# A two-layer diffusion backbone step on one core: layers written out, the close of a layer interleaved with the next projection, and its modulation computed by column strips ahead of time

## The chip, the cores and the metric

The kernel runs on one core of a Trainium2 chip, in float32 throughout but for a few counting matrices. The time is the device time of one launch in microseconds; three runs of the kernel before gave 2504.25, 2508.52 and 2509.11, median 2508.52. Engines: TensorE (PE in the profile) multiplies, VectorE (DVE), ScalarE (ACT) and GpSimd (POOL) work elementwise, SyncE (SP) only issues transfers. ACT and POOL issue transfers too.

## The reference

Two groups of tokens, 512 latent and 128 context, pass through two layers (DEPTH = 2). D_MODEL is 1024. What is computed, in the core of it:

```python
mod = silu(cvec) @ w_mod_l + b_mod_l            # 6 x 1024 values per conditioning vector
sh1, sc1, g1, sh2, sc2, g2 = split(mod, 6)
h = x * (1.0 + sc1) + sh1
qa,ka,va, qb,kb,vb, qc,kc,vc = split(h @ w_in_l)          # 1024 x 3840
oa, ob, oc = diff_attention, neighbourhood_attention, gqa  # latent reads cached context keys too
ga, gb, gc = split(sigmoid(h @ w_gate_l + b_gate_l), 3)
y = (ga * (oa @ w_br[0]) + gb * (ob @ w_br[1]) + gc * (oc @ w_br[2])) @ w_o
x = layernorm(alpha * x + g1 * y)
h2 = x * (1.0 + sc2) + sh2
m = grouped top-2 mixture of 16 experts: sum over chosen e of weight * (silu(h2 @ w1[e]) * (h2 @ w3[e])) @ w2[e]
x = layernorm(alpha * x + g2 * m)
```

Latent tokens are modulated by the vector c, context tokens by c_ctx. Outputs are x of both groups and the context keys and values of both layers.

## The kernel before, in words

The 640 tokens are five tiles of 128 (four latent, the fifth, CTX, context). All weights are cut into pieces of 1 MB (128 x 2048), laid out in DRAM in the order of use, and SyncE streams them into a ring of six slots (`ring`); PE takes each piece in that order and, with some of its matmuls, raises `freed`, which lets SyncE load the piece six places on. The order of work on every engine is that of the code: each engine has its own list, and semaphores (`wait_ge`) tie them.

A first block loads constants and all of x and computes the modulation's first four column groups of 512 (shift and scale of the first sublayer): `open_sp`, `open_pe`, `open_act`, `open_dve`. A group is eight matmuls with the conditioning `cs` as 32 columns of weights, in four column strips of PE's array; the strips hold four *parts of the sum over rows*, so a further matmul with `sel` (L457) adds and turns them into columns. Then a loop over layers (L542) runs one body twice, in blocks with barriers between them:

- `transpose_x` (L756) and `modulate` (L1140) make hT, the modulated transposed input, for all tiles; x is stored to `x_state`, its place is reused, and ACT waits for that store (L1121 is behind it).
- For each of three branches: `project` computes the chunks of the input projection tile by tile (PE line L718 is the shared matmul helper `mm`). Each chunk begins with one more 512-column group of the modulation (`mod_sum`), followed by `mod_rows`, a matmul with `sel` that sums the four strips into two rows, which ACT copies (L1130) and stores to `mrows` in DRAM. Then `attend`, with gate matmuls (`fill`) put between as filler by the table FILL, and `merge`.
- x and the rows come back from DRAM (POOL, L651 to L666) once branch 2's values are mixed. VectorE prepares G1, SH and SC (L1512 to L1519), PE does the output projection by tile, VectorE the residual, statistics and h2 (L1527 to L1537), PE transposes h2 and computes the router.
- Routing on VectorE (L1548 to L1588 up to the choice), rank counting by matmul (L1044), then 17 expert blocks in a pipeline: gather of tokens (POOL), w1, w3, SiLU, w2, store to `y_rows`.
- After a barrier and a possible loop over further blocks, a last block of the layer gathers both outputs of each token (L1794), weighs (L1815), adds (L1827), gates, normalises and, beside it, opens the modulation of `(layer + 1) % DEPTH`. After layer 1 it opens layer 0 again, which nobody reads. x is then stored in one transfer (L1852).

## Time and profile before

| | us |
|---|---|
| median of 3 runs | 2508.52 |
| the profiled execution | 2503.88 |
| its span, first to last instruction | 2502.2 |
| PE busy | 2218.6 (89%) |
| VectorE busy | 882.7 (35%) |
| ScalarE busy | 568.8 (23%) |
| mean granted clock of PE | 0.951 |

PE is the engine that is nearly always busy; an idle microsecond of another engine costs nothing unless PE waits for it. A float32 matmul shows as two instructions in the timelines (x16 for eight matmuls). In a row of a timeline the bracket is the idle time of the engine just before, and what ended it. The granted clock is 1.0 at 2.4 GHz and 0.5 at 1.2 GHz.

### The profile page before, as it was taken

Reading aid. Unit: us, or ns where it says so; the run is one execution under the profiler, and the core shown is the slowest. Engines: PE = TensorE matmul, PEld = TensorE weight load, DVE = VectorE, ACT = ScalarE, POOL = GpSimd, SP = SyncE. Lnnn points to the kernel's source line nnn. Section 1 sums busy time; section 2 is a strip of 40 time slices with the busy share of each in tenths; the row PEclk is TensorE's granted clock in tenths of the full one; section 3 lists DMA queues with packets and bytes.
Section 4 is the critical chain, followed back from the end, with each engine's and each line's share of the span. In section 5 each row is a group of like instructions: output and inputs, shape, how many; then the busy total and the mean of one; then the engine's idle time right before and its main releaser. Section 6 shows DMA issues by size and latency. Waiting matters only on the chain. (4 is left out here: it accounts for less than half of the span.)

```text
span 2502.2 us, 28473 instructions
## 1 busy us (share of the span) xinstructions
PE 2218.6 (89%) x11178; PEld 1408.7 (56%) x11178; DVE 882.7 (35%) x1532; ACT 568.8 (23%) x1040; POOL 242.4 (10%) x245
## 2 busy tenths in 40 slices
PE   3899999999989996999469999999999899969973
PEld 2347754566466643888234576446645665558851
DVE  0115510243543364331532253004435334553216
ACT  2013401142034201122221242113401440112112
POOL 0000010020100000010410001002101000001014
PEclk8999999999999997999679999999999999969985
DMA  8411031211210322799642202211122105059966
GB/s 311 197 78 55 35 105 74 103 47 54 87 68 18 140 105 105 274 364 369 263 186 87 90 34 72 118 72 62 41 88 86 35 18 210 34 192 357 360 267 257
DMA packets 59540, 345.12 MB, mean 138 GB/s; under 512 B 7056, under 2 KB 8208, under 8 KB 28880
## 3 DMA queue, kind: packets, MB, share of 16 engines
q1 hardware_dynamic: 35072, 249.04, 26.3%
q0 software_dynamic: 15744, 63.58, 6.7%
q10 hardware_dynamic: 8592, 30.68, 3.1%
q8 instruction: 91, 1.49, 0.2%
q14 instruction: 41, 0.34, 0.0%
HBM read 309.91 MB, written 37.55 MB: 139 GB/s over the span
## 5 line engine op out<-in xcount | busy, mean ns | idle before, releaser
L718 PE MATMUL ps<-ring,hT 128*128 128x512 f32 (+1 forms) x1280 | 530.1, 568 | 1.1 <-DMA ring<-in_wall 1.0
L718 PE MATMUL ps<-hT,ring 128*128 128x320 f32 x1536 | 464.6, 440 | 0.0
L718 PEld LDWEIGHTS ps<-ring,hT 128*128 128x128 f32 x1280 | 238.2, 190 | 265.9 <-issue 257.2
L718 PEld LDWEIGHTS ps<-hT,ring 128*128 128x128 f32 x1536 | 273.1, 190 | 98.4 <-issue 2.8
L718 PEld LDWEIGHTS ps<-zT,ring 128*128 128x128 f32 x2176 | 255.6, 195 | 18.4 <-issue 15.3
L718 PE MATMUL ps<-zT,ring 128*128 128x128 f32 x2176 | 260.0, 279 | 2.3 <-ACT zT L1283 2.3
L718 PE MATMUL ps<-R,ring 128*128 128x512 f32 (+1 forms) x768 | 211.1, 435 | 4.6 <-DVE zT L1506 3.2
L718 PEld LDWEIGHTS ps<-R,ring 128*128 128x128 f32 x768 | 117.0, 191 | 98.6 <-issue 92.5
L1221 ACT ACTIVATE R<-ps,nmax 128x640 f32<-128x640 f32 x128 | 100.4, 790 | 248.2 <-DVE nmax L1414 248.2
L1414 DVE TENSOR_REDUCE nmax<-ps 128x2 f32<-128x1280 f32 x64 | 95.5, 1491 | 151.4 <-PE ps L842 151.2
L718 PE MATMUL ps<-ring,zT 128*128 128x512 f32 x320 | 139.2, 594 | 3.7 <-DVE zT L1506 3.7
L1394 DVE TENSOR_REDUCE cmax<-ps 128x4 f32<-128x512 f32 x12 | 8.3, 692 | 349.6 <-PE ps L842 349.4
L842 PE MATMUL ps<-R 64*128 64x128 f32 (+3 forms) x992 | 127.5, 383 | 3.1 <-ACT R L1165 1.7
L718 PE MATMUL ps<-ring,R 128*128 128x512 f32 x272 | 122.5, 593 | 3.0 <-issue 3.0
L1237 ACT COPY R<-ps 128x512 f32<-128x512 f32 (+3 forms) x202 | 111.4, 552 | 33.0 <-PE ps L903 26.8
L1678 DVE TENSOR_TENSOR R<-R,ps 128x256 f32<-128x256 f32 x34 | 14.3, 421 | 285.5 <-ACT R L1301 285.5
L842 PEld LDWEIGHTS ps<-R 64*128 64x128 f32 x992 | 92.6, 187 | 37.8 <-issue 14.1
L718 PEld LDWEIGHTS ps<-ring,zT 128*128 128x128 f32 x320 | 60.2, 190 | 76.8 <-issue 72.7
L1183 ACT COPY R<-ps 128x512 f32<-128x512 f32 (+1 forms) x54 | 28.4, 526 | 303.4 <-PE ps L718 303.4
L903 PE MATMUL ps<-ident,R 128*128 128x128 f32 x680 | 91.2, 273 | 6.2 <-DVE R L1435 4.4
L903 PEld LDWEIGHTS ps<-ident,R 128*128 128x128 f32 x680 | 80.2, 141 | 29.2 <-DVE R L1435 6.4
L450 PE MATMUL ps<-ring,cs 128*32 128x512 f32 x192 | 39.1, 939 | 64.0 <-DMA ring<-in_wall 64.0
(195 smaller groups left out, 2012.4 us busy)
## 6 DMA issues: line engine op xcount, KB each, us to landing
ring<-in_wall SPq DMA_DIRECT2D x234, 1024.0 KB, 7.8
y_rows<-R ACTq DMA_DIRECT2D x34, 512.0 KB, 8.7
R<-mrows POOLq DMA_DIRECT2D x16, 512.0 KB, 22.2
R<-in_rows POOLq DMA_DIRECT2D x2, 3072.0 KB, 20.2
x_state<-R POOLq DMA_DIRECT2D x2, 2560.0 KB, 25.1
R<-x_state POOLq DMA_DIRECT2D x2, 2560.0 KB, 12.6
h_rows<-R ACTq DMA_DIRECT2D x10, 512.0 KB, 2.6
R<-in_bias POOLq DMA_DIRECT2D x8, 384.0 KB, 4.2
```

The lines of the kernel that those rows point to most:

```text
L450: last = nc.tensor.matmul(ps[32 * j:32 * j + 32, 6, :], cs[:, 4 * hf + j, :], w[:, j, :], start=hf == 0, stop=hf == 1)
L718: ins = nc.tensor.matmul(out, w, m, start=start, stop=stop, **kw)
L842: return nc.tensor.matmul(out, QT[lo:lo + 64, b, 128 * r:128 * r + 128], KT[lo:lo + 64, key_slot(br, b), k0:k0 + n], start=True, stop=True)
L903: last = nc.tensor.transpose(ps[:, 3 + c + k // 4, 128 * (k % 4):128 * (k % 4) + 128], P[:, i % 2, c, 128 * k:128 * k + 128], ident[:])
L1183: ch.step(nc.scalar.copy(dst, src), a_copy)
L1221: ins = nc.scalar.activation(dst, src, ACT.Exp, bias=nmax[:, n + a:n + a + 1], accum_out=rsum[:, n + a:n + a + 1])
L1237: ch.step(nc.scalar.copy(dst, src), a_pt)
L1394: ch.step(V_.tensor_reduce(m2[:, a, :].unsqueeze(2), s4[:, a], axis=AX.X, op=ALU.max), v_chain)
L1414: ch.step(V_.tensor_reduce(nmax[:, n:n + 2].unsqueeze(2), src, axis=AX.X, op=ALU.max, negate=True), v_max)
L1678: ch.step(V_.tensor_tensor(sig, sig, bank[:, 0], ALU.mult), v_chain)
```

## The change

1. *Layers written out.* `for layer in range(DEPTH)` in Python replaces the loop on the engines; the opening block and the closing block of a layer are gone. What they did stands at the head of the next layer's one big block. The final close is a block of its own, without a modulation.
2. *Modulation by column strips.* A piece of w_mod is now 128 rows by 2048 columns. The four strips of PE's array hold four different groups of 512 *columns*, and eight pieces sum over the rows in place. So no `mod_rows` and no `gsm` copy; ACT stores strips straight to `mrows`. Shift and scale of the first sublayer are one such group of eight pieces, turned into columns by four matmuls (`mod_turn`).
3. *Ahead of time.* Layer 1's first group is computed in layer 0: two pieces before the last transposition of h2, six behind the last router matmul. The first three pieces of layer 1's second group are preloaded.
4. *Close and projection interleaved.* In layer 1, for each tile: gather, weigh, add, normalise, transpose (`transpose_x(t + 1)` inside the matmuls of tile t), modulate, project V (V is now the first chunk of branch 0). The gain and offset of the norm are folded into the modulation columns (`mod_columns`), so x kept in `x_state` is normalised only, and VectorE applies gain and offset when it comes back.
5. *The opening of layer 0* loads x by tile on ACT's queue and modulates hT on VectorE in place.
6. *Other.* x has moved to the space of the gates (its reload waits for the end of `merge(2)`), and the second sublayer's shift and scale are prepared after tile 0's statistics (`second_modulation`). h2 comes by two fused steps without ACT. Sigmoid is replaced by Exp or Tanh. Ranks of routing are accumulated over tiles by matmul. Output x is stored by tile.

The diff, cut to its core:

```diff
-TAIL_FILL = (0, 0, 8)
+TAIL_FILL = (8, 0, 8)
-CHUNKS = {0: (0, 1, 2), 1: (3, 4, 5), 2: (6, 7)}
+CHUNKS = {0: (2, 0, 1), 1: (3, 4, 5), 2: (6, 7)}
+MOD_SPREAD = {0: ((0, 4, 4), (3, 3, 2)), 1: ((3, 3, 2), (3, 3, 2))}
...
+        def mod_strips(k, bank, w, first):
+            for j in range(STRIPS):
+                ins = first if j < STRIPS - 1 else nc.tensor.matmul
+                last = ins(ps[32 * j:32 * j + 32, bank, :], cs[:, k, :], w[:, 512 * j:512 * j + 512], start=k == 0, stop=k == KB - 1)
+            return last
+        def mod_turn(out):
+            for b in range(4):
+                last = nc.tensor.matmul(out[:, 8 * b:8 * b + 8], modraw[:, 128 * b:128 * b + 128], sel[:], start=True, stop=True)
+            return last
...
+        def fetch_and_scale(pool, ch):
+            for t in range(4):
+                fetch_outputs(pool, t)
+            scale_power(pool, ch, 0)
+            fetch_outputs(pool, 4)
+            for t in range(1, NT):
+                scale_power(pool, ch, t)
...
-        with nc.Fori(0, DEPTH) as layer:
+        for layer in range(DEPTH):
...
+                    for i in range(PRELOADED if layer else 0, n_pieces - 3):
+                        if i >= SLOTS:
+                            sp.wait_ge(freed, i - SLOTS + 1)
+                        lay, what = pieces[i]
+                        load(i, lay, WALL.index(what))
...
-                    pool.dma_start(x[:], A["x_state"].rearrange("t p n -> p t n")).then_inc(x_in, 16)
-                    pool.dma_start(rows[:], A["rows"][layer][:, 0:6]).then_inc(rows_in, 16)
+                    pool.dma_start(rows[:], A["rows"][layer]).then_inc(rows_in, 16)
...
+                    spread(G1, 0, g1_in)
+                    pool.wait_ge(v_z, 3 * KB)
+                    pool.dma_start(x[:], (A["x_state"] if layer else A["x"]).rearrange("t p n -> p t n")).then_inc(x_again, 16)
                     spread(SH, 1, g_in)
                     spread(SC, 2, g_in)
...
+                                        if layer:
+                                            pe.wait_ge(a_hT, KB * t + k + 1)
+                                        elif t == 0:
+                                            pe.wait_ge(v_hT, k + 1)
+                                        if layer and k == KB - 3 and t + 1 < NT:
+                                            transpose_x(t + 1, 4)
...
                     router(NT - 2)
+                    if not last_layer:
+                        pe.wait_ge(v_ln, 8)
+                        for k in range(2):
+                            mod_piece(k, 3)
                     transpose_h2(NT - 1)
                     router(NT - 1)
+                    if not last_layer:
+                        for k in range(2, KB):
+                            mod_piece(k, 3)
+                        pe.wait_ge(a_mod, n_mod[0])
+                        mod_turn(ps[:, 4, 384:512]).then_inc(pe_ext, 1)
...
+                    if layer == 0:
+                        act.dma_start(ident[:], A["ident"]).then_inc(ident_in, 16)
+                        for t in range(NT):
+                            act.dma_start(x[:, t, :], A["x"][t]).then_inc(xt_in[t], 16)
+                        act.dma_start(par[:], A["par"][0]).then_inc(par_in, 16)
+                        act.wait_ge(cs_in, 16)
+                        ch.step(nc.scalar.activation(cexp, cs[:], ACT.Exp, scale=-1.0), a_cs)
+                        act.dma_start(zf[:, 0:256 + 2 * NT], A["counting"]).then_inc(count_in, 16)
+                        for n, t in names:
+                            act.dma_start(t[:], A[n]).then_inc(consts_in, 16)
+                        for t in range(NT):
+                            act.wait_ge(pe_xT, 2 * t + 2)
+                            ch.step(nc.scalar.copy(hT[:, :, 128 * t:128 * t + 128], flat(4 * (t % 2), 1024)...), a_raw)
+                        keep_mod(6)
+                    else:
+                        gate_lambda()
+                        weigh(act, ch, 0)
+                        weigh(act, ch, 1)
+                        norm_tile(0)
+                        modulate(0)
...
                     for t in range(NT):
...
                         norm_stats(ch, t)
-                        norm_shift(dve, ch, t, 15)
-                        dve.wait_ge(a_ln, t + 1)
+                        if t == 0:
+                            second_modulation()
...
-                        ch.step(V_.tensor_tensor(h2[:, t % 2, :], x[:, t, :], SC[:, v, :], ALU.mult), v_chain)
-                        ch.step(V_.tensor_tensor(h2[:, t % 2, :], h2[:, t % 2, :], SH[:, v, :], ALU.add), v_h2)
+                        ch.step(V_.scalar_tensor_tensor(h2[:, t % 2, :], x[:, t, :], lnst[:, t, 12:13], SC[:, v, :], ALU.subtract, ALU.mult), v_chain)
+                        dve.wait_ge(g_rs, normed + t + 1)
+                        ch.step(V_.scalar_tensor_tensor(h2[:, t % 2, :], h2[:, t % 2, :], lnst[:, t, 15:16], SH[:, v, :], ALU.mult, ALU.add), v_h2)
```

How the order of instructions moves, at the places that matter. PE at the change of layer, before: what follows the last expert matmul and the skipped loop over further blocks, the opening of the next layer (the rows with `sel` turn a group) and the loop back.

```order
L1783 UNCONDITIONAL_BRANCH
L450 MATMUL ps<-ring,cs 32x512 x8
L457 MATMUL ps<-sel,R 128x2 x4
L450 MATMUL ps<-ring,cs 32x512 x8
L457 MATMUL ps<-sel,R 128x2 x4
L450 MATMUL ps<-ring,cs 32x512 x8
L457 MATMUL ps<-sel,R 128x2 x4
L450 MATMUL ps<-ring,cs 32x512 x8
L457 MATMUL ps<-sel,R 128x2 x4
L1775 UNCONDITIONAL_BRANCH
L542 REGISTER_ALU
L542 COMPARE_AND_BRANCH
```

Now (from the head of layer 1's block; L712 and L451 with `cs` are modulation pieces, L744 transposes x, L712 with `hT` projects V):

```order
L693 UNCONDITIONAL_BRANCH
L712 MATMUL ps<-ring,cs 32x512 x3
L451 MATMUL ps<-ring,cs 32x512
L712 MATMUL ps<-ring,cs 32x512 x3
L451 MATMUL ps<-ring,cs 32x512
L712 MATMUL ps<-ring,cs 32x512 x3
L451 MATMUL ps<-ring,cs 32x512
L744 MATMUL ps<-ident,R 128x128 x8
L712 MATMUL ps<-ring,hT 128x512 x5
L744 MATMUL ps<-ident,R 128x128 x8
L712 MATMUL ps<-ring,hT 128x512 x8
L744 MATMUL ps<-ident,R 128x128 x8
L712 MATMUL ps<-ring,hT 128x512 x8
```

The four modulation groups and the loop's branches are gone from between the layers; three pieces stand first, and each later tile's transposition lies five matmuls into the tile before it.

PE in layer 0 at the end of the output projection, before (L718 with `wr` is the router, L1011 transposes h2, L1044 counts ranks):

```order
L718 MATMUL ps<-ring,zT 128x512 x16
L1011 MATMUL ps<-ident,R 128x128 x8
L718 MATMUL ps<-wr,hT 128x16 x16
L1011 MATMUL ps<-ident,R 128x128 x8
L718 MATMUL ps<-wr,hT 128x16 x8
L1044 MATMUL ps<-selbf,lt 128x80
L1045 MATMUL ps<-selbf,ones 128x80
```

And now: the router of tiles 2 and 3, two modulation pieces, the last h2, its router, then the first of six pieces.

```order
L712 MATMUL ps<-wr,hT 128x16 x16
L712 MATMUL ps<-ring,cs 32x512 x3
L451 MATMUL ps<-ring,cs 32x512
L712 MATMUL ps<-ring,cs 32x512 x3
L451 MATMUL ps<-ring,cs 32x512
L1018 MATMUL ps<-ident,R 128x128 x8
L712 MATMUL ps<-wr,hT 128x16 x8
L712 MATMUL ps<-ring,cs 32x512 x3
L451 MATMUL ps<-ring,cs 32x512
L712 MATMUL ps<-ring,cs 32x512 x3
L451 MATMUL ps<-ring,cs 32x512
```

The pieces stand where PE waited for VectorE before.

VectorE at the start of the output projection, before (the ten 1024-wide rows, then the first of tile 0's residual, L1527 and L1528):

```order
L1514 TENSOR_TENSOR R<-R 128x1024
L1515 SCALAR_TENSOR_TENSOR R<-R 128x1024
L1517 TENSOR_TENSOR R<-R 128x1024
L1518 TENSOR_TENSOR R<-R 128x1024
L1519 TENSOR_TENSOR R<-R 128x1024
L1514 TENSOR_TENSOR R<-R 128x1024
L1515 SCALAR_TENSOR_TENSOR R<-R 128x1024
L1517 TENSOR_TENSOR R<-R 128x1024
L1518 TENSOR_TENSOR R<-R 128x1024
L1519 TENSOR_TENSOR R<-R 128x1024
L1527 SCALAR_TENSOR_TENSOR R<-ps,R 128x512
L1528 SCALAR_TENSOR_TENSOR R<-R 128x512
```

And now:

```order
L1612 TENSOR_TENSOR R<-R 128x1024 x2
L1639 SCALAR_TENSOR_TENSOR R<-ps,R 128x512
L1643 SCALAR_TENSOR_TENSOR R<-R 128x512
L1639 SCALAR_TENSOR_TENSOR R<-ps,R 128x512
L1643 SCALAR_TENSOR_TENSOR R<-R 128x512
L438 BN_STATS R<-R 128x6 x2
L439 BN_AGGR R<-R 128x2
L440 TENSOR_SCALAR small<-R 128x1
L1621 TENSOR_TENSOR R<-R 128x1024
L1622 SCALAR_TENSOR_TENSOR R<-R 128x1024
L1624 TENSOR_TENSOR R<-R 128x1024
L1625 TENSOR_TENSOR R<-R 128x1024
```

The ten rows have moved behind the residual and the statistics of tile 0 (L438 to L440), in front of its h2.

## Rows read from the trace of the kernel before

**Rows 1.** The page, part 1: busy us (share) and instructions of PE.

```profile
PE 2218.6 (89%) x11178; PEld 1408.7 (56%) x11178; DVE 882.7 (35%) x1532; ACT 568.8 (23%) x1040; POOL 242.4 (10%) x245
```

**Rows 2.** Windows view, stretch: length, busy per engine (instructions), PEclk, DMA share, GB/s.

```profile
892.04:1001.41 109.37, 86.26 (x297) 46.76 (x297) 64.71 (x126) 12.78 (x12) 6.30 (x8) 0.87 0.22 80
1001.41:1205.90 204.49, 201.83 (x1430) 168.24 (x1430) 56.49 (x131) 39.93 (x50) 18.54 (x16) 0.98 0.84 317
1205.90:1291.36 85.46, 27.75 (x137) 13.90 (x136) 43.64 (x56) 26.66 (x33) 35.17 (x22) 0.58 0.67 257
2424.46:2502.20 77.74, 20.22 (x97) 8.32 (x96) 42.11 (x50) 15.30 (x15) 34.85 (x21) 0.54 0.64 247
...
10.00:20.00 10.00, 1.93 (x8) 0.20 (x8) 0.45 (x3) 0.00 (x0) 0.00 (x0) 1.00 1.01 419
```

**Rows 3.** PE timeline, opening: start, duration, line, out<-in, count, idle before it.

```profile
65.95 7.54 PE L718 MATMUL ps<-ring,hT 128*128 128x512 f32 x16 [0.98 <-DMA ring<-in_wall]
80.80 1.87 PE L718 MATMUL ps<-R,sel 128*2 128x512 f32 x2 [7.32 <-ACT R L1121]
82.60 8.30 PE L718 MATMUL ps<-ring,hT 128*128 128x512 f32 x16
```

**Rows 4.** ACT timeline, opening (ACTq: its DMA issues).

```profile
14.66 8.80 ACTq L512 DMA_DIRECT2D iota<-in_iota  x1
23.98 0.59 ACT L465 COPY R<-ps 128x512 f32<-128x512 f32 x1 [20.57 <-issue]
```

**Rows 5.** DMA issues of the span: transfer, count, KB each, us to landing.

```profile
R<-mrows POOLq DMA_DIRECT2D x16, 512.0 KB, 22.2
R<-x_state POOLq DMA_DIRECT2D x2, 2560.0 KB, 12.6
h_rows<-R ACTq DMA_DIRECT2D x10, 512.0 KB, 2.6
R<-in_x ACTq DMA_DIRECT2D x1, 2560.0 KB, 23.5
```

**Rows 6.** PE timeline at the layer change.

```profile
1279.51 2.40 PE L756 MATMUL ps<-ident,R 128*128 128x128 f32 x10 [12.11 <-issue]
1291.36 1.92 PE L718 MATMUL ps<-ring,cs 128*32 128x512 f32 x16 [1.83 <-ACT hT L1140]
1300.28 1.02 PE L718 MATMUL ps<-R,sel 128*2 128x512 f32 x2
1301.23 7.13 PE L718 MATMUL ps<-ring,hT 128*128 128x512 f32 x16
```

**Rows 7.** POOL, ACT and DVE timelines at the layer change.

```profile
1212.50 0.98 POOL L1794 DMA_INDIRECT zT<-y_rows,yrow  x1 [41.32 <-issue]
...
1219.55 1.15 ACT L1815 ACTIVATE zT<-zT,R 128x1024 f32<-128x1024 f32 x1 [12.56 <-DMA R<-y_rows,yrow]
...
1223.52 1.28 DVE L1827 SCALAR_TENSOR_TENSOR zT<-R,zT 128x1024 f32<-128x1024 f32 x1 [1.50 <-ACT zT L1815]
1227.36 1.42 DVE L395 BATCH_NORM_STATS2 R<-R 128x6 f32<-128x512 f32 x2
```

**Rows 8.** PE and DVE timelines, start of the output projection of layer 0.

```profile
892.04 27.73 PE L718 MATMUL ps<-ring,zT 128*128 128x512 f32 x64 [1.87 <-DVE zT L1506]
919.61 1.04 PE L1011 MATMUL ps<-ident,R 128*128 128x128 f32 x8
...
897.06 1.23 DVE L1517 TENSOR_TENSOR R<-R 128x1024 f32<-128x1024 f32 x1
915.56 1.23 DVE L1537 TENSOR_TENSOR R<-R 128x1024 f32<-128x1024 f32 x1
```

**Rows 9.** PE timeline, end of the output projection and routing, layer 0.

```profile
975.57 1.97 PE L1011 MATMUL ps<-ident,R 128*128 128x128 f32 x8 [4.04 <-DVE R L1537]
991.57 0.25 PE L1044 MATMUL ps<-selbf,lt 128*128 128x80 bf16 x1 [9.34 <-DVE selbf L1588]
```

**Rows 10.** SyncE timeline, last DMA issue of the span.

```profile
2493.88 0.41 SPq L1852 DMA_DIRECT2D out_y<-R  x1
```

840 lines of the change are left out of this document (426 added, 414 removed).

## The prediction

> **What bounds the kernel now.** I read the page's busy shares first, then cut the span into stages with the windows view, then read each engine's timeline where the cuts show idle time. TensorE (PE) is busy 2218.6 us of 2502.2 [rows 1], so only 283.6 us are to be had unless its work shrinks. In the expert stage it is busy 201.83 of 204.49 us, and the transfers move 317 GB/s there with the engines 84% busy [rows 2]: full, and untouched by the change. The idle time lies in four places: the opening, where the first projection starts at 65.95 us and the second tile only at 82.60 after a 7.32 us wait for ScalarE [rows 3]; the change of layer, 85.46 us with PE busy for 27.75; routing, where PE is busy 86.26 of 109.37 us; and the last 77.74 us, where the 20.22 us of PE work is a modulation for a third layer that is never run [rows 2]. The granted clock is 0.58 and 0.54 in the two gaps against 0.98 in the expert stage [rows 2], that is mostly 1.2 GHz: what PE starts after a gap runs slow at first.
>
> **The opening.** Before, subtracting one steady tile (7.13), one row sum (0.95) and one modulation sum (1.92, durations from [rows 6]) from 82.60 gives 72.6 us as the moment from which the stream would have run without loss. Now: nothing waits for all of x or for a barrier, but 15 transfers are issued on ScalarE's queue before its first copy of x, where there were 12 before its first copy; that copy began at 23.98, after 20.57 us without work, 8.80 of them inside one issue [rows 4]. I put it at 25. Then PE has three tiles to transpose (2.0 each on the slow clock [rows 9]: 6) and seven of the eight modulation pieces left (0.96 each fast, from 1.92 for 16 instructions [rows 6], up to twice that slow; I take 1.2: 8.4), and ScalarE's copy (0.6 [rows 4]), the turn into columns (1.9, priced as the 2-instruction row sum at 1.87 [rows 3]), and small column operations (about 1.7, no row, from six operations at a few tenths): 43.6, say 44. Gain 28.6. Bounds: the data needed is 8.4 MB of modulation, 2.6 MB of x and 1.2 MB of constants, 12.2 MB at 419 GB/s [rows 2] or 29 us, plus start and tail, 37 at best; 52 if ring slots are freed late behind the blocked copies. So 20 to 36.
>
> **Row sums.** Each of eight chunks per layer had a matmul that summed four partial rows; the strips are now whole sums. Start to start it takes 0.95 (1300.28 to 1301.23 [rows 6]), sixteen of them: 15.2, all on PE's path. The modulation sums themselves stay (32 instructions of the same form per 2048 columns) and only change places.
>
> **Second modulation.** This one goes the other way. x now shares its space with the gates, so its reload is issued after the last merge step, with the shift and scale rows queued behind it, and ten 1024-wide VectorE operations on them come after tile 0's statistics. Before they ran at once from 892 on, and h2 of tile 0 was ready at 916.79, 2.8 us before PE wanted it (915.56 + 1.23 against 919.61 [rows 8]). Count from the first output matmul, 892.04: the second half of tile 0 ends at +13.9 (half of 27.73, by two tiles, [rows 8]); add two operations (1.4), statistics (1.9, from 1.42 [rows 7] and two small ones), ten at 1.26 (1.23 and its gap [rows 8]: 12.6), two for h2 (2.6): +32.4. PE wants it at +27.6. It waits 5 us, and restarts on the slow clock (a transposition block is 1.97 after a 4.04 us wait [rows 9] against 1.04 [rows 8]), which I price at 2.5 with the matmuls behind. The reload (12.6 [rows 5]) fits in front of the +13.9; rows from mrows took 22.2 behind 9 MB, now behind 2.6 MB; if they took that again they would land near +24, 7 us late. Per layer 7.5, bounds 0 and 15: cost 15, bounds 0 and 30.
>
> **End of projection and routing.** VectorE now subtracts the mean and scales in two fused steps, so ScalarE's pass over x and its two hops leave the chain of h2 (about 2.1 of the 4.04 us wait [rows 9]); Exp in place of Sigmoid drops a table load, and fewer group operations and rank sums by matmul save some 2.6 more of the 9.34 [rows 9] and what follows. Layer 1 gets this whole, with some slow-clock time back: 8. In layer 0 the eight modulation pieces of layer 1 are put into these waits. Only two are in the ring; six must be loaded once the output weights are freed, and 6.3 MB at 419 GB/s is 15 us, plus about 1.5 of start and finish (h rows: 2.6 us for 0.5 MB [rows 5], which moves in 1.3). They end about 17 us after the loads start, then copy and turn (2.5): just where the rank matmul starts before, 991.57. So layer 0 gains 1. Together 9, bounds 2 and 14.
>
> **The change of layer.** Before, 85.46 us from the last expert matmul to the first modulation sum of layer 1 [rows 2]. Now the gathers start as before (1212.50, +6.6), the first pair is usable at +13.65 (1219.55) [rows 7], but SyncE issues three ring loads at once and three more as PE uses the preloaded pieces. With equal shares the first pair is 2.6 us later and each next one 5 apart; say +17. Scaling 1.15, combine 1.28, two steps of 1.23, statistics 1.9 [rows 7 and 8], the power and the mean (0.8, no row), ScalarE's normalising pass (1.15 like the scaling), half a transposition and one modulate put the first projection matmul near +29 to +31; I take 30. Tile 1 then needs VectorE 6.1 and ScalarE about 5 us per tile against PE's 8.2 (7.13 + 1.04), so the supply keeps up after one wait of some 2.3. Four more transpositions inside the stream cost 4.2; three modulation pieces are done inside the gap, 2.8 saved. 30 + 2.3 + 4.2 - 2.8 = 33.7: gain 51.8, bounds 42 and 58.
> The trace shows that shares need not be equal: x (2.6 MB) took 23.5 us [rows 5] beside ring loads, 112 GB/s of 419. The Trainium skill, DMA: Bandwidth & Descriptors, section Queues, rings and completion order, says that a DMA engine takes turns between queues by whole packets, not by bytes; with 8 KB ring rows against 4 KB gathered rows that gives gathers a third, the trace agrees, and the first rival below is what it would make of this place.
>
> **The end.** Before, 77.74 us after the last expert matmul [rows 2]. Now the dead modulation, its barrier and the 2.5 MB store in one piece (2493.88 to the end, 8.3 [rows 10]) go; per tile VectorE does combine, gate, add, statistics and two fused steps, 1.28 x 3 + 1.23 x 2 + 1.9 + gaps 0.5 = 8.7. First combine at +15.5 (the pair usable at +13.65 as at the layer change, scaling 1.15, and under 1 us for the 1 MB of final rows loaded beside), five tiles 43.5, last store 0.4 + 2.6 [rows 5] + 1: 63. Gain 14.7, bounds 8 and 17.
>
> **Sum.** 28.6 + 15.2 - 15 + 9 + 51.8 + 14.7 = 104.3 from 2502.2: 2397.9 of span. The profiled execution before took 2503.88, 1.7 over its span, and the median of the runs is 4.6 above that (lowest 0.4 above); with half of it, 2401. The rest (Tanh for Sigmoid in the experts, V before Q and K, eight fill matmuls moved to the last K unit, layers written out) I cost at nothing: VectorE is 28% busy under the experts [rows 2], the fills are the same 128 per branch. Were V-first to expose the last K copy, it would be 1 us per layer.
>
> **Rivals.**
> *Starved handover.* While 6.3 MB of ring loads last (some 20 us at 307 GB/s) a pair of gathers, 1 MB, comes every 9.4 us at x's 112 GB/s in place of 5. Two pairs are then late by 4.4 each: the first projection is at +34 and the next tile waits as much again, and the slow clock lasts longer; together 14 more: 2415. For it: the 23.5 us [rows 5]. Against: the ring has only 6 slots, so its lead ends after 6.3 MB. 0.17.
> *Second modulation hidden.* Rows land early and the wait is under 2 us per layer, without slow clock; for it, the 2.8 us of slack before. Against: ten operations in VectorE's line. 2401 - 13 = 2388. 0.15.
> *The opening stays blocked.* ScalarE's queue holds it until x is in (27 us) and the ring, its slots freed late, runs behind: first projection at 55, gain 17.6: 2412. 0.13.
> *The experts turn transfer-bound, slower than before.* Layer 0 enters its experts with the ring behind, and the stage needs 4.2 MB per expert in 11.7 us. The price is 34 periods; the gains of 104 are eaten from 3.1 us per period on, for instance 14.9 us each: 2401 + 110 = 2511. Against: bytes and slots are unchanged and 84% is not full; ring loads run at 2.5 us per MB when not held. 0.02.
> *It does not do what it says*: the projection of layer 1 still waits for the whole close, because the tiles' scaling, normalising and modulation queue on ScalarE in one order. Then the first tile comes after all five, 20 later: 2421. 0.06.
>
> **How the numbers follow.** The forecast, 2401, has 0.47. Ends of all terms together give 2367 and 2450; they will not all fall one way, and 8 in 10 of the cases above lie in 2378 to 2426. What this kernel's measurement can tell from no change is 0.2%, 5 us; every case but the transfer-bound one is far beyond it: faster 0.97, same 0.01, slower 0.02.
>
> **What would show it.** Right: the first ring-by-hT matmul at 40 to 48 us; no matmul of sel by R with 512 columns; one wait of PE of 3 to 8 us for h2 before the first transposition block of each output projection; the first projection of layer 1 28 to 33 us after the last expert matmul of layer 0; an expert stage of 204 to 206 us; an end of 60 to 65 us. Wrong: new waits of PE for the ring in routing or the experts, waits of several us in more than one tile at the layer change, or a granted clock near 0.5 through the first projected chunk, which would cost up to 7 us a tile.

## The result, and the profile after

The changed kernel takes 2436.11 us (median of 4 runs, 2433.51 to 2438.39), the kernel before 2508.82 (2504.25 to 2509.3): a ratio of 0.9714, 95% interval 0.9697 to 0.9731. It is faster by 72.7 us, where the prediction's sum had 104.3. The time lies 35 us above the predicted 2401 and 10 us above the range. The profiled execution has a span of 2435.8 us, PE busy for 89% of it as before, with 38.7 us less work [rows 1]:

```profile
PE 2179.9 (89%) x11018; PEld 1395.5 (57%) x11018; DVE 888.5 (36%) x1519; ACT 530.9 (22%) x1004; POOL 215.4 (9%) x231
```

To see where a forecast of a sum went wrong, both spans are cut at the same events, with the forecast of each stage beside them. The events are the first projection matmul, the first matmul of the output projection, the first expert matmul and the end of the last, per layer; the "before" of the first two lines counts from 72.6 us, as the prediction did, and in layer 1 from the first modulation sum of the first chunk (1291.36), for the same reason. "Forecast" is before with the prediction's terms put in (the sixteen row sums are 7.6 a layer).

| stage, us | before | forecast | measured | missed by |
|---|---|---|---|---|
| opening | 72.6 | 44 | 41.3 | -2.7 |
| layer 0, first to output projection | 819.4 | 811.8 | 830.8 | +19.0 |
| layer 0, output projection and routing | 112.5 | 119.0 | 123.7 | +4.7 |
| layer 0, experts | 201.4 | 201.4 | 200.5 | -0.9 |
| last expert matmul to first projection | 85.5 | 30 | 32.9 | +2.9 |
| layer 1, first to output projection | 819.4 | 815.5 | 825.0 | +9.5 |
| layer 1, output projection and routing | 112.3 | 111.8 | 118.0 | +6.2 |
| layer 1, experts | 201.4 | 201.4 | 201.1 | -0.3 |
| end | 77.7 | 63 | 62.6 | -0.4 |

The new gaps are small, and most are in places where the prediction had seen none. In the windows view (length, busy time per engine, PEclk, DMA share, GB/s) of output projection and routing, the change of layer and the end, which answer to the rows in [rows 2]:

```profile
872.07:981.10 109.03, 98.47 (x353) 49.46 (x354) 56.59 (x90) 5.88 (x7) 11.45 (x11) 0.92 0.39 153
1196.29:1229.14 32.85, 7.03 (x32) 2.59 (x33) 11.39 (x18) 5.26 (x7) 10.74 (x11) 0.62 0.84 333
2373.22:2435.80 62.58, 0.00 (x1) 0.00 (x0) 40.28 (x45) 6.75 (x6) 18.60 (x15) 0.54 0.40 151
```

PE's timeline in the first projection of layer 0 (start, duration, line, out<-in, count, idle before it and its releaser; L774 transposes a Q or K unit):

```profile
38.36 1.06 PE L457 MATMUL ps<-sel,R 128*128 128x8 f32 x8 [0.79 <-ACT R L1151]
41.27 37.47 PE L712 MATMUL ps<-ring,hT 128*128 128x512 f32 x80 [1.85 <-DVE hT L1405]
...
87.27 16.07 PE L712 MATMUL ps<-ring,hT 128*128 128x512 f32 x32 [4.95 <-DMA ring<-in_wall]
...
131.79 8.80 PE L712 MATMUL ps<-ring,hT 128*128 128x512 f32 x16 [2.53 <-DMA ring<-in_wall]
140.43 0.60 PE L774 MATMUL ps<-ident,R 128*128 128x128 f32 x4
140.87 7.03 PE L712 MATMUL ps<-ring,hT 128*128 128x512 f32 x16
```

The stream starts at 41.27, where [rows 3] had 65.95 and 82.60. But it stops twice for weights, 4.95 and 2.53 us. After the second stop eight matmuls (x16) take 8.80 us, after the next unit 7.03. Only what comes right behind the wait is slow.

The same at the change of layer, PE and then ScalarE (ACT L493 weighs a gathered tile, L1178 normalises, L1172 modulates, L1246 copies V):

```profile
1227.38 1.97 PE L744 MATMUL ps<-ident,R 128*128 128x128 f32 x8 [19.52 <-ACT R L1178]
1229.14 5.71 PE L712 MATMUL ps<-ring,hT 128*128 128x512 f32 x10
1236.74 1.07 PE L744 MATMUL ps<-ident,R 128*128 128x128 f32 x8 [1.88 <-issue]
1237.65 7.03 PE L712 MATMUL ps<-ring,hT 128*128 128x512 f32 x16
1246.24 1.07 PE L744 MATMUL ps<-ident,R 128*128 128x128 f32 x8 [1.56 <-issue]
```

```profile
1215.80 1.15 ACT L493 ACTIVATE zT<-zT,R 128x1024 f32<-128x1024 f32 x1 [12.61 <-DMA R<-y_rows,yrow]
1223.20 1.15 ACT L493 ACTIVATE zT<-zT,R 128x1024 f32<-128x1024 f32 x1 [6.24 <-DMA R<-y_rows,yrow]
...
1235.40 1.24 ACT L1178 ACTIVATE R<-R 128x1024 f32<-128x1024 f32 x1 [1.73 <-DVE R L1393]
1237.47 3.90 ACT L1172 ACTIVATE hT<-ps,modcol 128x128 f32<-128x128 f32 x8 [0.83 <-PE ps L744]
1241.40 0.59 ACT L1246 COPY R<-ps 128x512 f32<-128x512 f32 x1
1242.02 1.15 ACT L493 ACTIVATE zT<-zT,R 128x1024 f32<-128x1024 f32 x1
1244.90 1.24 ACT L1178 ACTIVATE R<-R 128x1024 f32<-128x1024 f32 x1 [1.73 <-DVE R L1393]
```

Where [rows 6] had one transposition for all of x at 1279.51 and a projection from 1301.23, tile 0 is projected from 1229.14. ScalarE then needs 9.50 us per tile (1235.40 to 1244.90): 6.88 of work and 2.6 of waiting. PE needs 7.03 + 1.07 less overlap, 7.9, and waits for the difference ahead of three tiles (1.88, 1.56 and 1.56 us; the last one it has in time).

The output projection, VectorE (L1639 and L1643 residual of a half tile, L1621 the first of ten rows of the second modulation, L1654 h2) and PE in layer 0, then PE in layer 1:

```profile
872.05 2.48 DVE L1612 TENSOR_TENSOR R<-R 128x1024 f32<-128x1024 f32 x2
884.80 0.69 DVE L1639 SCALAR_TENSOR_TENSOR R<-ps,R 128x512 f32<-128x512 f32 x1 [10.27 <-DMA R<-in_x]
...
891.21 1.23 DVE L1621 TENSOR_TENSOR R<-R 128x1024 f32<-128x1024 f32 x1
...
905.13 1.28 DVE L1654 SCALAR_TENSOR_TENSOR R<-R 128x1024 f32<-128x1024 f32 x1
```

```profile
906.47 1.97 PE L1018 MATMUL ps<-ident,R 128*128 128x128 f32 x8 [4.97 <-DVE R L1654]
...
2089.71 1.97 PE L1018 MATMUL ps<-ident,R 128*128 128x128 f32 x8 [7.85 <-DVE R L1654]
```

In [rows 8] the ten rows ran from 892 on and h2 was ready in time. Now VectorE stands idle for 10.27 us and does them afterwards.

### The profile page after: what moved, and what is told of

Its sections match the earlier page's. It is cut to its first block and busy times, and to the rows that moved or that the text cites. A ratio compares the mean times of both kernels' runs of the same rounds, so it can differ in the third digit from the quotient of the medians.

```text
span 2435.8 us, 27121 instructions
## 1 busy us (share of the span) xinstructions
PE 2179.9 (89%) x11018; PEld 1395.5 (57%) x11018; DVE 888.5 (36%) x1519; ACT 530.9 (22%) x1004; POOL 215.4 (9%) x231
## 5 line engine op out<-in xcount | busy, mean ns | idle before, releaser
L712 PE MATMUL ps<-ring,hT 128*128 128x512 f32 (+1 forms) x1280 | 536.9, 575 | 13.5 <-DMA ring<-in_wall 7.9
L712 PE MATMUL ps<-hT,ring 128*128 128x320 f32 x1536 | 465.2, 440 | 0.0
L712 PEld LDWEIGHTS ps<-ring,hT 128*128 128x128 f32 x1280 | 241.6, 193 | 274.7 <-issue 258.0
L712 PEld LDWEIGHTS ps<-hT,ring 128*128 128x128 f32 x1536 | 273.3, 190 | 97.8 <-issue 2.5
L712 PEld LDWEIGHTS ps<-zT,ring 128*128 128x128 f32 x2176 | 254.5, 194 | 18.4 <-issue 15.3
L712 PE MATMUL ps<-zT,ring 128*128 128x128 f32 x2176 | 258.9, 279 | 2.3 <-ACT zT L1349 2.3
L712 PE MATMUL ps<-R,ring 128*128 128x512 f32 (+1 forms) x768 | 211.1, 435 | 4.6 <-DVE zT L1606 3.2
L712 PEld LDWEIGHTS ps<-R,ring 128*128 128x128 f32 x768 | 116.9, 191 | 98.6 <-issue 92.5
L712 PE MATMUL ps<-ring,zT 128*128 128x512 f32 x320 | 143.9, 610 | 3.7 <-DVE zT L1606 3.7
L712 PE MATMUL ps<-ring,R 128*128 128x512 f32 x272 | 122.5, 593 | 3.0 <-issue 3.0
L1793 DVE SCALAR_TENSOR_TENSOR R<-R,ps 128x256 f32<-128x256 f32 x34 | 14.3, 421 | 280.3 <-ACT R L1367 280.3
L712 PEld LDWEIGHTS ps<-ring,zT 128*128 128x128 f32 x320 | 62.1, 196 | 79.9 <-issue 75.7
L1246 ACT COPY R<-ps 128x512 f32<-128x512 f32 (+1 forms) x54 | 28.5, 527 | 348.4 <-PE ps L712 348.3
L942 PE MATMUL ps<-R 128*64 128x128 f32 x1088 | 73.5, 279 | 12.9 <-ACT R L1299 12.9
## 6 DMA issues: line engine op xcount, KB each, us to landing
R<-in_x ACTq DMA_DIRECT2D x5, 512.0 KB, 13.5
```

What stands on the lines that cost most here:

```text
L712: ins = nc.tensor.matmul(out, w, m, start=start, stop=stop, **kw)
L942: last = nc.tensor.matmul(ps[64 * a:64 * a + 64, 5, 128 * r:128 * r + 128], V[:, kt, 64 * vh:64 * vh + 64], PT[:, a, 128 * j:128 * j + 128 ...
L1246: ch.step(nc.scalar.copy(dst, src), a_copy)
L1793: ch.step(V_.scalar_tensor_tensor(sig, sig, 1.0, bank[:, 0], ALU.add, ALU.mult), v_chain)
```

## The experiments

Every edit is made on the changed kernel. Ratios are to the kernel before, with 95% interval; the changed kernel itself is at 0.9714 and, run again beside e9 and e10, at 2434.85 us, 0.9709 (0.9694 to 0.9725).

### e1_second: the second modulation into VectorE's idle time

```
                     spread(G1, 0, g1_in)
+                    spread(SH, 1, g_in)
+                    spread(SC, 2, g_in)
                     pool.wait_ge(v_z, 3 * KB)
                     pool.dma_start(x[:], ...).then_inc(x_again, 16)
-                    spread(SH, 1, g_in)
-                    spread(SC, 2, g_in)
...
+                    second_modulation()
                     dve.wait_ge(x_again, 16)
...
-                        if t == 0:
-                            second_modulation()
```

> Edit, alone on the changed kernel: the spreads of the second shift and scale are issued before POOL waits for the last z block, and VectorE does the ten operations of the second modulation before it waits for the x that is loaded again. Theory A (the ten operations sit behind the x load, 12.6 us of VectorE in series with a 10.27 and a 9.05 us idle wait): they move into that idle time, h2 of tile 0 is ready about 10 us sooner in each layer, the PE waits for h2 (4.97 and 7.85 us) and the cold transpositions after them go, about 6 to 9 us per layer; time about 2421, 2417 to 2425. Rival B (what lies between output projection and router is set by VectorE's sum of work or by the x load itself, not by this order): the waits move to later tiles and the time stays within 4 us of 2436. Rival C: the spreads only come so late that VectorE waits for them instead, no gain.

Measured 2418.48 us (5 runs, 2415.05 to 2423.26), 0.9647 (0.963 to 0.9664): 17.6 us less. Theory A. VectorE's timeline shows the ten rows from 874.34 to 886.9, with no wait for x behind them, and PE's transposition of the first h2 no longer waits and takes 1.04 us in place of 1.97:

```profile
885.68 1.22 DVE L1626 TENSOR_TENSOR R<-R 128x1024 f32<-128x1024 f32 x1
886.94 0.69 DVE L1640 SCALAR_TENSOR_TENSOR R<-ps,R 128x512 f32<-128x512 f32 x1
```

```profile
871.84 29.43 PE L712 MATMUL ps<-ring,zT 128*128 128x512 f32 x64 [1.87 <-DVE zT L1606]
901.11 1.04 PE L1018 MATMUL ps<-ident,R 128*128 128x128 f32 x8
```

From output projection to rank matmul the stage falls from 109.0 to 101.7 us in layer 0 and from 107.1 to 96.4 in layer 1. The order of these ten operations had cost 7.3 and 10.7 us.

### e2_late, e3_233, e12_800: where the modulation pieces of layer 0 stand

```
-MOD_SPREAD = {0: ((0, 4, 4), (3, 3, 2)), 1: ...}
+MOD_SPREAD = {0: ((0, 0, 0), (3, 3, 2), (5, 3)), 1: ...}   # e2_late, groups in branches 1 and 2
+MOD_SPREAD = {0: ((2, 3, 3), (3, 3, 2)), 1: ...}           # e3_233
+MOD_SPREAD = {0: ((8, 0, 0), (3, 3, 2)), 1: ...}           # e12_800
```

> Edit, alone: layer 0 takes its two further modulation groups in the projections of branches 1 and 2 (3, 3, 2 and 5, 3 pieces before the chunks) and none in branch 0. Theory A (in the changed kernel the four pieces ahead of the second and third chunk fill the ring beside the two pieces held, so the next chunk's weights land late: waits of 4.95 and 2.53 us and a slow clock after each): both waits and the slow matmuls go, 10 to 13 us less, about 2424 (2421 to 2428). The cost of the modulation matmuls themselves (0.86 us a piece) only moves. Rival B (the projection of branch 0 is slow for want of clock after the opening, whatever the ring does): within 4 us of 2436. Rival C (the five pieces before branch 2's first chunk are loaded late in their turn): a ring wait of 3 to 5 us there, half of the gain lost, about 2430.

Measured 2427.21 us (5 runs), 0.9679 (0.9665 to 0.9693): 8.9 less, theory A's direction and a little short of its 10 to 13, and the pieces' own 6.9 us (8 x 0.86) are still there, in branch 2. No ring wait is left in the first branch's projection. One of 2.29 us stands at the second branch's third chunk, and a ring wait of 3.50 us in the opening, which the changed kernel's trace has at 0.56, put the first projection at 44.6. That start moves by itself: the seven other traces with the changed kernel's opening and projection of the first branch (c_after, e1, e4, e5, e6, e7, e9) have it between 41.96 and 44.44.

> Edit, alone: the modulation pieces in branch 0 of layer 0 stand 2, 3, 3 before the chunks where the changed kernel has 0, 4, 4. Theory A (ring full): the waits inside the projection shrink to under 1 us each, but the first chunk starts 5 to 7 us later, since two pieces load ahead of its weights; net 3 to 6 us less, about 2431. Rival B (the ring is not the cause): 5 us more, 2441, for the later start.

Measured 2424.68 us (5 runs), 0.9684 (0.9666 to 0.9703): 11.4 less, more than theory A gave. The first projection starts 4.3 us later, and first to output projection takes 813.9 us in place of 830.8. Of these 16.9 us, 1.7 are two pieces that stand ahead of it now, and 1.6 lie behind the projection, where the changed kernel's trace has a stretch of slow matmuls behind a wait for ScalarE that most other traces don't have (e8 and e9 do). The remaining 13.5 lie between the first projection matmul and the last but one Q/K transposition (128.4 us against 113.1): 7.0 of ring waits, 3.5 of slow matmuls behind them and 2.9 of slow matmuls in the first chunk. In the eight traces with the changed kernel's order in it this stretch takes 123.5 to 128.4 us, 126.1 in the mean, so against the mean the gain is 11.3. The windows view over the projection of branch 0, the changed kernel first, then two finer cuts of it (PEclk is the third number from the end):

```profile
41.27:78.74 37.47, 37.47 (x84) 16.24 (x88) 5.76 (x16) 5.94 (x12) 0.00 (x0) 0.92 0.26 108
78.74:110.00 31.26, 26.31 (x84) 11.09 (x84) 4.46 (x8) 1.18 (x2) 0.55 (x1) 0.89 0.53 210
110.00:131.79 21.79, 19.26 (x78) 8.32 (x77) 4.47 (x8) 2.96 (x5) 0.00 (x0) 1.00 0.18 67
131.79:152.00 20.21, 20.20 (x49) 9.24 (x50) 4.46 (x8) 1.18 (x2) 0.00 (x0) 0.92 0.57 241
```

```profile
50.00:78.74 28.74, 28.74 (x71) 12.44 (x74) 0.00 (x0) 2.34 (x4) 0.00 (x0) 1.00 0.03 12
110.00:125.69 15.69, 15.69 (x50) 7.43 (x52) 4.47 (x8) 1.55 (x3) 0.00 (x0) 1.00 0.00 0
```

And e3_233:

```profile
45.55:80.20 34.65, 34.65 (x84) 15.24 (x88) 1.87 (x9) 2.55 (x5) 0.00 (x0) 1.00 0.31 129
80.20:110.00 29.80, 29.33 (x92) 12.73 (x86) 6.70 (x12) 1.78 (x3) 0.55 (x1) 1.00 0.47 185
110.00:131.00 21.00, 21.00 (x76) 9.29 (x75) 3.44 (x7) 2.97 (x5) 0.00 (x0) 1.00 0.44 173
```

With two pieces of work just ahead of it the first chunk runs at 2.4 GHz throughout here (1.00), where the changed kernel's first chunk, behind waits of 0.79 and 1.85 us, has 0.92. That this is the pieces' doing is not shown: e8 and e10 have the same two pieces there, and their first chunks took 36.2 and 36.3 us, e3's 34.6, the changed kernel's 37.5. The two finer cuts show the full ring: while PE works through a chunk the transfers stand still (12 and 0 GB/s), and they run at 241 when the weights are needed already. e3's ring waits there are 0.47 us.

> Edit, alone on the changed kernel (undoes 'ahead of time and spread' for layer 0): all eight pieces of the next modulation group stand before the first chunk of layer 0, none between chunks. The pieces land about 2.5 us apart. Theory A (the opening is bound by the ring's loads once ScalarE is free, and ring room is what costs later): the first projection starts 18 to 22 us later, near 61, the waits of 4.95 and 2.53 us and the slow clock inside the projection go (11 us, as e3 and e2 showed); net 6 to 11 us more, 2442 to 2446. Rival B (the loads hide behind the wait for the modulation columns): the first projection starts under 10 us later and the time is below 2435.

Measured 2435.33 us (5 runs), 0.9704 (0.9686 to 0.9721): the same time as the changed kernel, between the two theories. The mechanism is A's, since the first projection starts at 60.39, behind pieces that land one by one:

```profile
47.88 1.08 PE L712 MATMUL ps<-ring,cs 128*32 128x512 f32 x3 [1.42 <-DMA ring<-in_wall]
50.36 1.07 PE L712 MATMUL ps<-ring,cs 128*32 128x512 f32 x3 [0.55 <-DMA ring<-in_wall]
52.84 1.07 PE L712 MATMUL ps<-ring,cs 128*32 128x512 f32 x3 [0.55 <-DMA ring<-in_wall]
...
60.39 50.30 PE L712 MATMUL ps<-ring,hT 128*128 128x512 f32 x112 [0.64 <-DMA ring<-in_wall]
```

The sum in the expectation was wrong. I had left out that the eight pieces' matmuls leave the stream (6.9 us), and priced ring and clock at 11. First to output projection takes 809.4 us, 21.4 less, of which 6.9 are those and 1.6 the slow stretch behind the projection; the 12.9 left are ring waits and slow clock (10.7 against the mean of the eight traces). So all that the changed kernel wins in the opening by putting these pieces off, 19.1 us, it pays back in the projection.

### e4_fill: the gate matmuls ahead of the last K unit

```
-TAIL_FILL = (8, 0, 8)
+TAIL_FILL = (0, 0, 8)
...
-    ((0, 6, 0),) + 6 * ((0, 4, 3),) + 4 * ((0, 4, 2),) + 6 * ((0, 4, 3),) + ((0, 6, 0),),
+    ((4, 6, 0),) + 16 * ((0, 4, 3),) + ((0, 6, 0),),
```

> Edit, alone: the eight gate matmuls that the change put ahead of the last K unit of branch 0 go back to where the kernel before has them (4 ahead of slot 0, and 4 slots with 3 after the transpositions in place of 2). Theory A (those matmuls cover no wait of their size before the attention, and four slots now wait 0.8 us each for want of them): 1 to 3 us less per layer, about 2432 (2429 to 2435). Rival B (they cover the copy and transposition of the last K unit, a wait of 3 to 4 us opens in their place in each layer): 2 to 6 us more, about 2440.

Measured 2430.49 us (5 runs, 2427.23 to 2436.77), 0.9701 (0.9684 to 0.9719): 5.6 less in the medians, but the intervals overlap, so the time alone does not settle it. The traces do: from the last but one Q/K transposition to the first mixing of values it is 16.75 us in place of 19.35, and every trace of a kernel with the eight matmuls ahead has 19.35 or 19.36 there, in both layers. Theory A, with 2.6 us per layer. Eight matmuls (4.47 us together) covered a wait that with the old order is 0.28 us long:

```profile
166.80 0.66 PE L774 MATMUL ps<-ident,R 128*128 128x128 f32 x4 [0.28 <-ACT R L1246]
```

### e5_ring: the ring's loads behind the gathers

```
+                        if layer and i in (3, 5):
+                            sp.wait_ge(yt_in[i - 3], 32)
```

> Edit, alone on the changed kernel: in layer 1 SyncE loads its fourth and fifth ring piece only when the first pair of gathered outputs is in, and the sixth when the third pair is in; in the changed kernel all five loads are issued at the start of the layer, beside the gathers. Theory A (the gathers share the DMA engines with five ring pieces, so pair 0 takes 12.9 us from the start of its gather): pair 0 lands 3 to 6 us sooner and the first projection of layer 1 starts 3 to 6 us sooner (27 to 30 us after the last expert matmul, against 32.85); time 2431 to 2433. Rival B (the gathers are set by POOL's issue of the descriptors, 1.3 us each, or by their own latency): within 1.5 us there and 2 us of 2436 in all. Rival C: the weights come too late in their turn, a ring wait opens ahead of the first projection, 2 to 6 us slower.

Measured 2427.79 us (5 runs), 0.9669 (0.9647 to 0.9691): 8.3 less, more than expected. The last expert matmul ends at 1197.36 here, and the first projection starts at 1222.64, 25.3 us later in place of 32.9. ScalarE's timeline:

```profile
1210.93 1.15 ACT L493 ACTIVATE zT<-zT,R 128x1024 f32<-128x1024 f32 x1 [6.67 <-DMA R<-y_rows,yrow]
1213.94 1.15 ACT L493 ACTIVATE zT<-zT,R 128x1024 f32<-128x1024 f32 x1 [1.86 <-DMA R<-y_rows,yrow]
1219.58 1.24 ACT L1180 ACTIVATE R<-R 128x1024 f32<-128x1024 f32 x1 [4.50 <-DVE R L1395]
```

Pair 0 is usable 13.6 us after the last expert matmul (19.5 in the changed kernel, 13.65 before [rows 7]) and pair 1 3.0 us after it (7.4). No weight is late in the first chunk.

### e6_two, e7_half, e9_nmr: ScalarE's period

> Leaves out: in layer 1 the first modulation takes the gain and offset of column 0 for all 8 column blocks, so that ScalarE does two operations of 128 x 512 in place of eight of 128 x 128 per tile. Theory A (ScalarE's period of 9.49 us per tile sets the first chunk of layer 1, PE needs 7.9): with modulate at about 1.3 us in place of 3.90 the waits of 1.88, 1.56 and 1.56 us ahead of the transpositions go, and the first tile is ready 1 to 2 us sooner; 5 to 7 us less, about 2430. Rival B (the period is set by VectorE's combine chain or by the gathers, ScalarE only has much to do): the tile period stays above 9 us and the time within 2 us of 2436.

```
+                        if layer:
+                            for k in range(2):
...
+                                nc.scalar.activation(hT[:, 4 * k:4 * k + 4, ...], ps[:, 4 + k, :]..., ACT.Identity,
+                                                     scale=modcol[:, KB:KB + 1, v], bias=modcol[:, 0:1, v]).then_inc(a_hT, 4)
```

Measured 2432.36 us (5 runs, 2427.04 to 2434.95), 0.9689 (0.9665 to 0.9713). The medians give 3.7 less, the ratios 6; the interval overlaps the changed kernel's. In the trace modulate takes 1.64 us in place of 3.90 and the tile period falls from 9.50 to 8.57 (1231.64 to 1240.21), the waits from 1.56 to 0.64. They do not go: ScalarE still waits 1.73 us for the mean in every tile, and 1.35 opens before its copy of V. So its work was a part of the period and not the whole: neither theory in full. The time alone cannot tell this run from the changed kernel.

> Edit, alone: in layer 1 VectorE modulates the upper four column blocks of tiles 2, 3 and 4 (four operations of 128 x 128 from PSUM each), ScalarE the rest. Theory A (ScalarE sets the period): the waits ahead of the transpositions of tiles 3 and 4 go and that of tile 2 stays; 2 to 4 us less, about 2433. Rival B (VectorE's own chain of about 7 us per tile then holds the modulation back): the waits turn into waits for VectorE of 2 us or more at tile 2, no gain or up to 3 us more.

```
+SHARED = (2, 3, 4)
...
+                                for u in (SHARED[:-2] if t < NT else SHARED[-2:]):
+                                    dve.wait_ge(pe_xT, 2 * u + 2)
+                                    for k in range(KB // 2, KB):
+                                        ch.step(V_.tensor_scalar(hT[:, k, ...], ps[:, 5, ...], modcol..., modcol..., ALU.mult, ALU.add), v_hT)
```

Measured 2440.72 us (5 runs, 2439.77 to 2442.22), 0.9725 (0.9703 to 0.9746): 4.6 us more than 2436.11, and rival B had up to 3. Its mechanism is what the trace shows. VectorE reaches tile 2's half only after its last sums, at 1257.62, and PE waits in the middle of the tile:

```profile
1258.09 1.70 PE L719 MATMUL ps<-ring,hT 128*128 128x512 f32 x2 [4.97 <-DVE hT L1436]
```

> Edit, alone on the changed kernel: at the change of layer VectorE forms the negated mean of tile t right after its sums, ahead of the combination of tile t+1 (it then waits about 0.8 us for POOL's power). Theory A (ScalarE's period of 9.49 us holds 1.73 us of waiting for that value and 6.9 us of work, so most of it is order, not work): the wait goes, the period falls to about 8 us, the PE waits of 1.88, 1.56 and 1.56 us shrink under 0.5 us, and tile 0 is ready 0.5 to 1.5 us sooner; 4 to 6 us less, about 2431. Rival B (ScalarE's work sets the period whatever the order): within 1.5 us of 2436.

```
                             if t < NT:
                                 combine(dve, ch, t)
-                            if t:
-                                negated_mean(t - 1)
-                            if t < NT:
                                 add_outputs(ch, t)
+                                negated_mean(t)
```

Measured 2428.4 us (median of 6 runs, one of them at 4307.29 us; the median of the other five is 2427.05), 0.9675 (0.9659 to 0.9691): 6.5 less than 2434.85. Theory A. PE does not wait for ScalarE after tile 0, and the tile period is 7.8:

```profile
1229.48 6.30 PE L712 MATMUL ps<-ring,hT 128*128 128x512 f32 x10
1235.61 1.04 PE L744 MATMUL ps<-ident,R 128*128 128x128 f32 x8
1236.49 7.03 PE L712 MATMUL ps<-ring,hT 128*128 128x512 f32 x16
1243.38 1.07 PE L744 MATMUL ps<-ident,R 128*128 128x128 f32 x8
```

ScalarE's work is as before, 3.90 us of modulate included. Not its amount alone but a wait for a tiny VectorE operation, queued behind 1.3 us of the next tile's combination, had set the period. The first chunk of layer 1 falls from 44.8 to 39.9 us, 4.9 less. First to output projection falls by 6.8, from 825.0 to 818.2 us, but 1.7 of that are 32 instructions far behind, which run slow in the changed kernel's trace and not in this one (last section).

### e8_all, e10_best, c_after: the edits together

> Edits together on the changed kernel: second modulation ahead of the x load (e1: 17.6 us measured), pieces 2, 3, 3 in layer 0 (e3: 11.4), the gate matmuls back (e4: 5.6), the ring loads of layer 1 after the gathers (e5: 3 to 6), VectorE's share of the modulation (e7: 2 to 4). Theory A (the terms lie at different places and add): 38 to 44 us less than 2436, about 2395 (2390 to 2400), which would be near what was forecast for the changed kernel. Rival B (they overlap, as e3 and e4 both shorten the first branch of layer 0 and e5 and e7 the same handover): 28 to 34 us less, about 2405.

Measured 2404.7 us (5 runs), 0.9578 (0.9556 to 0.9599): 31.4 less, in rival B's range. But the trace has e7's wait of PE for VectorE in it again, 4.97 us, with slow matmuls after it (first to output projection of layer 1 takes 829.6 us), so overlap was not the cause that it showed.

> Edits together on the changed kernel: second modulation ahead of the x load, pieces 2, 3, 3 in layer 0, the gate matmuls back, the ring loads of layer 1 after the gathers, the negated mean ahead of the next combination; without VectorE's share of the modulation (e7, 4.6 us slower; e8 with it 2404.7). Theory A (e8's missing gain was that share, about 5 to 6 us, and the new order gives 4 to 6 more): 2392 to 2397. Rival B (the terms overlap beyond that): 2400 to 2404.

> The changed kernel as it is, on the same chip as e9 and e10: 2436 (2432 to 2440) by every theory; it gives the base that the others are compared with.

e10_best measured 2391.19 us (5 runs, 2390.1 to 2395.71), 0.9533 (0.9519 to 0.9548), c_after 2434.85 (5 runs): 43.7 less than the changed kernel and 4.7% less than the kernel before. Theory A, just under its range. Alone, the five edits gave 16.4, 10.2, 4.4, 7.1 and 6.5 us against 2434.85, together 44.6: they add, as far as intervals of some 4 us either way for each of them can tell. The first projection of layer 1 starts right behind a transposition that waited 11.06 us, and is not interrupted:

```profile
1200.81 1.97 PE L746 MATMUL ps<-ident,R 128*128 128x128 f32 x8 [11.06 <-ACT R L1180]
1202.58 6.58 PE L714 MATMUL ps<-ring,hT 128*128 128x512 f32 x10
1209.00 1.04 PE L746 MATMUL ps<-ident,R 128*128 128x128 f32 x8
```

## Why the prediction was wrong

It was right in sign and on most steps, and wrong above all in what it cost at nothing. The terms below are in microseconds of span, where the miss is 37.9 (35 in the medians). By the prediction's own steps:

- **Opening: right.** ScalarE's first copy of x started at 23.66 (forecast 25), the turn at 38.36, the first projection at 41.27 in place of 44. The count of transfers was misread (16 now and 11 before on ScalarE's queue, not 15 and 12). The other traces with this opening start between 41.96 and 44.44, so the 2.7 us to the good are chance in part.
- **Experts and end: right.** 200.5 and 201.1 us for 201.4, and 62.6 for 63. No sum of row strips is left in the trace.
- **"The rest ... I cost at nothing": the step that failed**, and it failed by 18.7 of the 37.9 us. The spread of pieces in layer 0 (0, 4, 4) was read as work that "only changes places"; I counted its matmuls and not its slots. Two slots are held by the chunk in work, four by pieces, and the next chunk's weights find none. That cost 13.5 us in the changed kernel's trace by e3 and 12.9 by e12 (11.3 and 10.7 against the mean of eight traces): 7.0 of ring waits, 3.5 of slow matmuls behind them, and 2.9 of slow matmuls in the first chunk, which are not shown to come from the ring. The fill matmuls, "the same 128 per branch", are the same number in a worse place: 2.6 us in each layer (e4, by its traces).
- **Change of layer: the start nearly right, the supply wrong.** First projection at +32.9 against 30, in the bounds. The slip was shares: I put pair 0 at +17 and the later pairs 5 us apart; pair 0 came at +19.5 and pair 1 7.4 later. From pair 0 to the first projection it was 13.3 us for the 13 that were taken, though the terms listed come to some 10: the hops between the engines were allowed for but not shown. A pair of 1.05 MB in 7.4 us is 142 GB/s of the 415 that all transfers move there, a third. SyncE's queue moves 7.3 KB a packet in that stretch (6.29 MB in 864), the gathers' queue 3.6 KB (5.24 MB in 1440), so turns by whole packets would give the gathers just that. The Trainium skill, DMA: Bandwidth & Descriptors, section Queues, rings and completion order, states such turns, and the prediction drew the same third from it for its first rival; the trace here agrees. Taking the loads away gave back 7.6 us (e5). And "ScalarE about 5 us per tile" was wrong: 6.88 of work, since I took modulate as a single pass where it is eight operations of 0.49, and 2.6 of waits. That "the supply keeps up after one wait" was therefore false, 1.88, 1.56 and 1.56 us in turn. The cure was in the order and not in the work (e9, 4.9 us in the first chunk).
- **Second modulation: right in mechanism and place, a little small.** Forecast 7.5 us a layer, e1 shows 7.3 and 10.7. In layer 0 the wait of 4.97 us meets the forecast of 5 in part by luck: PE's first matmuls were slow (29.43 us where the forecast took 27.73), so that h2 was ready at +34.3 in place of +32.4 and PE came for it at +29.4 in place of +27.6. In layer 1 PE was in time, and two more operations of 1.23 us, which the term had not counted, stand between the landing of x and the residual. That the wait could be avoided altogether, since VectorE had 10 us idle in front of it, the prediction did not ask.
- **End of projection and routing: forecast 9 us of gain, measured about 1.** Layer 1 gained 5.0 for 8, layer 0 lost 3.9 where 1 was to be won; the working is below.
- **Sum.** By its own working it gives 2401.9 (2397.9 + 1.7 + half of 4.6), not 2401; this changes nothing.
- **Rivals.** The starved handover named the right mechanism, gathers beside ring loads, and priced it too high: 9.4 us a pair, 14 us in all, where pair 1 took 7.4 and the first projection came 2.9 late. No other rival occurred, and none looked for ring room inside a projection, where the largest part of the loss lay.
- **Signs.** All but one of the signs of being right came true (the first projection at 41.27, no sum of strips, waits for h2 of 4.97 and 7.85 us, +32.9, an end of 62.6), and the expert stage, counted as in [rows 2], took 203.6 and 204.2 us for 204 to 206. They look where gains were claimed, and so they could not show the loss. Of the signs of being wrong, ring waits in routing did appear (0.48, 1.42 and 1.42 us).

For routing the account is only argued from the traces. Without the second modulation's cost layer 0's stage is 116.4 us (123.7 - 7.3) against 112.5 before and layer 1's 107.3 (118.0 - 10.7) against 112.3. In layer 1 the waits ahead of the last h2 and of the rank matmul fell from 4.04 and 9.34 us to 2.24 and 7.96, 3.2 where 4.7 had been forecast. In layer 0 the loss has two places. The rank matmul comes 2.2 us later than before (101.7 us after the first output matmul in e1, 99.5 before): the last of the modulation pieces is in 19.4 us after their loads start, where 17 had been forecast. And PE waits 6.3 us for the first gather of tokens, 3.5 before and 2.4 in layer 1. The transfer engines are full in that wait (413 GB/s, against 159 before and 162 in layer 1), with the expert weights that queued behind the modulation pieces, so the ring's loads probably stand in the gather's way as they do at the change of layer. No run moved them; that stays open.

The ledger: ring and clock in layer 0's first branch 13.5, fills 5.2, slow stretches that some traces have and others don't 3.3 (1.6 in layer 0, 1.7 in layer 1), ScalarE's order 4.9, the start of layer 1 2.9, second modulation 3.0, routing 7.9, less 4.3 for stages that went better, are 36.4 of 37.9 us. Routing is what its two stages leave over when the second modulation is taken out, so the sum tests the other terms and not this one.

## What to carry to other kernels

When work is moved into a stream that is fed by a ring, count the slots that it holds at the moment when the next weights must be asked for, not only its matmuls; here eight pieces of 0.86 us cost 11 to 13 us more in waits and clock. Where an engine's period per tile is above its work, look for the small operation that it waits for and what is queued ahead of that, before splitting the work. And put operations that need no late transfer ahead of the wait for it.

## What the runs showed of the hardware

The clock after a short wait is not the same each time. In the changed kernel's trace the same 32 instructions behind the same wait of 1.87 us took 14.00 us in layer 0, with a granted clock of 1.00, and 15.70 in layer 1, with 0.89:

```profile
620.46 14.00 PE L712 MATMUL ps<-ring,hT 128*128 128x512 f32 x32 [1.87 <-DVE zT L1606]
1801.19 15.70 PE L712 MATMUL ps<-ring,hT 128*128 128x512 f32 x32 [1.87 <-DVE zT L1606]
```

At the second ring wait of layer 0, where the granted clock behind 2.53 us was 0.81, 16 instructions took 7.10 or 7.11 us behind waits of 2.37, 2.40, 2.42 and 2.47 us (e4, e5, e7, c_after), 8.80 behind 2.49, 2.53 and 2.84 (e6, changed kernel, e9), and 8.77 behind 3.99 (e1). At the first one 32 took 17.02 us behind 3.18 (c_after) and 15.67 behind 4.44 (e9). Such a place can so cost 1.7 us or nothing, and traces of the same code differ by it.

Small operations are dear: eight ScalarE operations of 128 x 128 take 3.90 us and two of 128 x 512 on the same data 1.64, 0.38 us for each operation more; four of 128 x 128 on VectorE take 1.75 (e7). While PE waited for them a ring piece of 1 MB came every 2.48 us (e12), 423 GB/s.
